# Weight sums of the seven-product groups made in device memory by adding transfers and streamed as pieces, with six groups in each of five down stages

## The chip, the cores and the metric

One core of one Trainium2 chip runs the whole program as a single launch. The metric is the device time of the program in microseconds, the median of several runs. PE is TensorE (its weight loads are listed as PEld), DVE is VectorE, ACT is ScalarE, POOL is GpSimd, SP is the engine that issues most transfers. L941 is line 941 of the kernel before; the changed kernel has other line numbers.

## The reference, cut to what matters

Two transformer blocks on 256 tokens of width 2048, all in float32. The parts that the change touches are the last matrix products of the two feed-forward layers:

```python
# first block, hidden width 8192
h = h + jnp.square(jax.nn.relu(hn @ ffn_w1[i])) @ ffn_w2[i]
...
# second block, hidden width 5632
gate, val = jnp.split(c, 2, axis=-1)        # c: causal convolution of h @ w_up
return (jax.nn.silu(gate) * val) @ w_down
```

Around them stand an attention layer with compression at the start (stages `vs` to `wo`), a gated product (`proj`, `gate`) and a sliding-window attention (`v2` to `wo2`).

## The kernel before

**Precision.** Each float32 operand is split into a high part (the value cast to `fp32r`) and a low part (the value minus its high part). A product of two tiles is three matmuls of 128x512: high by high, high by low, low by high (`product`, L941 to L943). For weights ACT writes the high part (L2157) and DVE the low part (L1307).

**The weight stream.** All weights lie in device memory as `wstream`, a row of 512 KB pieces (128 partitions x 1024 floats). SP loads piece i into one of four `raw` slots (L557) as soon as `lo_ready` says that the low part of piece i-4 is written. ACT casts it to one of four `wboth` slots as soon as `piece_used` says that PE is through with piece i-4; DVE then writes the low part and raises `lo_ready`, for which PE waits. So a piece passes SP, ACT, DVE and PE in this order, on each engine in the order of the stream.

**The stages.** The first feed-forward layer runs in four chunks of 2048 hidden units, c = 0 to 3. Stage `ff{c}` makes 16 hidden tiles from 32 pieces (four passes `it` of four tiles, `units`, L607 and L615; a tile takes two pieces). Stage `fd{c}` multiplies these 16 tiles by 2048 rows of the second weight (32 pieces, each one hidden tile's 128 rows by 1024 columns). The second layer has `up0`, `dn0`, `up1`, `dn1`, `up2`, `dn2`, with 16, 16 and 12 hidden tiles.

**What each hidden tile passes in an `ff` stage.** DVE reduces the two halves of the bank to `z` (L1338), POOL multiplies by the norm factors (L2661, called a take below), ACT applies relu (L2373) and writes the square's high part to H (L2375), POOL squares again (L2708) and writes the low part (L2711). On ACT the casts of the next two pieces stand behind relu and square of a tile; on DVE the reduction of a tile stands between two low parts.

**The seven-product groups.** A down stage is worked in two column halves (`cp` 0 and 1) of 16 pieces. In `plain` a piece costs four products (two token halves by two column halves of 512). Two neighbouring pieces, hidden tiles 2m and 2m+1, cost eight products plainly; a group (`group`) does them with seven, as Strassen's and Winograd's scheme does for a 2x2 block product. It needs sums of the four 128x512 weight tiles (`Tsum`) and sums of the hidden tiles (`mix`, L2746 to L2750 on POOL, high part L2411 on ACT, low part L2756 on POOL). Of the pair's first piece only half is split, since the other half enters in sums alone. Before the change four sums per group are made by DVE or POOL from `raw` (L1777 and L1779, or L2736 and L2738; then L1785 and L1787), cast by ACT (L2418, L2420) and lowered by DVE (L1794). `fd0` to `fd2` have two groups in each column half (m = 3 and 5), `dn0` and `dn1` two and three (m = 4, 6 and m = 2, 4, 6): 22 groups in all. `fd3` and `dn2` have none.

```python
FIRST = Pairing(((3, 5), (3, 5)), sides=12, mains=17, last_sides=28)
SECOND = Pairing(((4, 6), (2, 4, 6)), sides=14, mains=16, last_sides=32)
```

## Time and profile before

| | before |
|---|---|
| median of three runs | 2194.44 us (2193.75 to 2196.51) |
| the profiled execution's own time | 2195.73 us |
| its span in the profile | 2193.9 us |
| PE busy | 2180.1 us, 99% |
| DVE, ACT, POOL busy | 71%, 52%, 32% |
| share of packets of the weight stream's queue | 55.7% of 16 DMA engines |

The profile is of one execution. A busy PE is counted with modelled ends that overlap, so PE's pace is read from the distance of one start to another, not from a matmul's duration. An entry such as `[2.57 <-ACT wboth L2157]` says how long the engine was idle before the instruction and what ended it.

### The profile page before, as it was taken

The numbers are of one execution on the slowest core, as the hardware profiler recorded it, in microseconds if no ns is written. First come the engines' busy times: TensorE is split into PE (matmuls) and PEld (weight loads), VectorE is DVE, ScalarE is ACT, GpSimd is POOL, SyncE is SP. The second block draws the span as 40 slices with busy tenths as digits, with TensorE's granted clock in tenths as the row PEclk, the third lists the DMA queues.
The fourth block names the chain that finished last, engine by engine and source line by source line (L and its number), as shares of the span: only waits on it lengthen the run. The fifth ranks groups of instructions, "written<-read, shape, count | busy, mean of one in ns | idle before, by whom it ended". The sixth has DMA issues, their size and how long they took to land.

```text
span 2193.9 us, 34076 instructions
## 1 busy us (share of the span) xinstructions
PE 2180.1 (99%) x11511; PEld 1862.4 (85%) x11511; DVE 1566.5 (71%) x2187; ACT 1133.5 (52%) x1720; POOL 711.8 (32%) x625
## 2 busy tenths in 40 slices
PE   9999999999999999999999999999999999999998
PEld 7888988888888888888888887788888888888887
DVE  6876767558657757755878667567778777787775
ACT  6445555545445545454556455465455455554553
POOL 3202320361362263153000033005554355533531
PEclk9999999999999999999999999999999999999999
DMA  7665335556556556566565654545555665555664
GB/s 250 231 224 171 116 130 181 174 184 211 191 182 209 192 184 207 202 194 197 177 199 188 225 171 137 192 163 182 189 195 185 202 198 192 188 191 197 200 207 149
DMA packets 118084, 414.35 MB, mean 189 GB/s; under 512 B 12896, under 2 KB 18048, under 8 KB 117472
## 3 DMA queue, kind: packets, MB, share of 16 engines
q1 hardware_dynamic: 111600, 401.37, 55.7%
q10 hardware_dynamic: 6384, 11.70, 1.7%
...
q14 instruction: 43, 0.35, 0.0%
...
## 4 chain that ended last, share of the span: by engine, by line
PE 93%; DVE 4%; ACT 1%; DMA 1%; POOL 1%; issue 1%; SPq 0%; DVEq 0%; ACTq 0%; POOLq 0%
PE bank L607 33%; PE bank L615 17%; PE bank L941 6%; PE bank L943 6%; PE bank L942 6%; PE bank L664 2%; PE bank L666 2%; PE bank L665 2%; DVE wboth L1307 2%; PE bank L1269 1%; PE bank L1267 1%; PE bank L1268 1%; PE bank L740 1%; PE bank L1202 1%; PE bank L777 1%; PE bank L917 1%
## 5 line engine op out<-in xcount | busy, mean ns | idle before, releaser
L1307 DVE TENSOR_TENSOR wboth<-raw,wboth 128x1024 fp32r<-128x1024 f32 (+1 forms) x756 | 953.8, 1267 | 468.1 <-ACT wboth L2157 459.8
L2157 ACT CAST wboth<-raw 128x1024 fp32r<-128x1024 f32 (+1 forms) x756 | 773.0, 1034 | 469.3 <-PE bank L943 123.3
L607 PE MATMUL bank<-A,wboth 128*128 128x512 f32 x2928 | 705.4, 392 | 0.5 <-DVE wboth L1307 0.3
L607 PEld LDWEIGHTS bank<-A,wboth 128*128 128x128 f32 x2928 | 536.8, 188 | 105.3 <-issue 1.3
L615 PEld LDWEIGHTS bank<-A,wboth 128*128 128x128 f32 x2928 | 376.7, 191 | 14.8
L615 PE MATMUL bank<-A,wboth 128*128 128x256 f32 x2928 | 384.0, 283 | 0.0
L941 PE MATMUL bank<-wboth,H 128*128 128x512 f32 x508 | 197.8, 389 | 1.2 <-DVE wboth L1307 1.2
L943 PE MATMUL bank<-wboth,H 128*128 128x512 f32 x508 | 197.6, 389 | 0.0
L942 PE MATMUL bank<-wboth,H 128*128 128x512 f32 x508 | 197.6, 389 | 0.0
L2661 POOL TENSOR_TENSOR PT<-z,rs 128x256 f32<-128x256 f32 x88 | 92.5, 1052 | 263.4 <-DVE z L1338 261.3
L2661 POOL TENSOR_TENSOR bias<-z,rs 128x256 f32<-128x256 f32 x64 | 104.7, 1635 | 197.9 <-DVE z L1338 109.4
L1338 DVE TENSOR_REDUCE z<-bank 128x256 f32<-128x512 f32 x172 | 117.6, 685 | 12.2 <-PE bank L607 12.1
L2373 ACT ACTIVATE Sm<-bias 128x256 f32<-128x256 f32 x64 | 26.7, 418 | 171.2 <-POOL bias L2661 171.2
L941 PEld LDWEIGHTS bank<-wboth,H 128*128 128x128 f32 x508 | 95.4, 188 | 21.8 <-DVE wboth L1307 2.0
L943 PEld LDWEIGHTS bank<-wboth,H 128*128 128x128 f32 x508 | 95.4, 188 | 19.8
L942 PEld LDWEIGHTS bank<-wboth,H 128*128 128x128 f32 x508 | 95.4, 188 | 19.7
L2766 POOL TENSOR_TENSOR x<-x,Sm 128x512 f32<-128x512 f32 x18 | 35.4, 1995 | 206.8 <-DVE x L1841 137.6
L2611 ACT ACTIVATE PT<-PT,par 128x256 f32<-128x256 f32 x88 | 44.8, 509 | 98.0 <-POOL PT L2661 98.0
L2661 POOL TENSOR_TENSOR kT<-z,rs 128x256 f32 (+1 forms) x12 | 11.3, 946 | 248.8 <-DVE z L1338 248.8
L2077 DVE SCALAR_TENSOR_TENSOR Sm<-PT,par 128x256 f32<-128x256 f32 x88 | 50.4, 573 | 51.7 <-ACT PT L2611 51.7
L2805 POOL TENSOR_TENSOR bias<-Sm 128x256 f32<-128x256 f32 x44 | 72.4, 1645 | 39.6 <-DVE Sm L2080 39.3
L607 PE MATMUL bank<-H,wboth 128*128 128x512 f32 x320 | 79.1, 394 | 0.0
...
## 6 DMA issues: line engine op xcount, KB each, us to landing
raw<-wstream SPq DMA_DIRECT2D x756, 512.0 KB, 3.4
bias<-bias_rows ACTq DMA_DIRECT2D x6, 512.0 KB, 5.4
...
pA<-bias_rows ACTq DMA_DIRECT2D x2, 512.0 KB, 6.9
...
```

The lines of the kernel that those rows point to most:

```text
L607: last = nc.tensor.matmul(bank(j)[:, :], whi[:, s, cols(i)], moving(j, k), start=(k == 0), stop=(k == K - 1))
L615: last = nc.tensor.matmul(bank(j)[:, 0:S], wlo[:, s, cols(i)], moving(j, k)[:, 0, :], start=False, stop=False)
L941: nc.tensor.matmul(bank[:, :], a_hi, w_hi, start=start, stop=False)
L942: nc.tensor.matmul(bank[:, :], a_hi, w_lo, start=False, stop=False)
L943: return nc.tensor.matmul(bank[:, :], a_lo, w_hi, start=False, stop=stop)
L1307: V.tensor_tensor(wlo[:, s, 0:w], raw[:, s, 0:w], whi[:, s, 0:w].bitcast(F32), ALU.subtract).then_inc(lo_ready, 1)
L1338: V.tensor_reduce(dst(j) if dst else z[:, (z0 + j) % 4, :], bank[:, :].rearrange("p (h c) -> p c h", h=2), AX, ALU.add).then_inc(z_ready, 1)
L2077: V.scalar_tensor_tensor(tA[:, slot, :], ub[:, slot, 1:S + 1], w[1], c0[:, slot % 2, :], ALU.mult, ALU.add).then_inc(up_step, 1)
L2157: C.copy(whi[:, s, 0:w], raw[:, s, 0:w]).then_inc(hi_ready, 1)
L2611: C.activation(c0[:, j % 2, :], ub[:, j % 4, 0:S], ACT.Copy, scale=par[:, ds(PO["conv"][0] + 3 * (2 * t0 + j), 1)]).then_inc(up_c0, 1)
L2661: return lambda zz: G.tensor_tensor(dst, zz, by, ALU.mult)
L2805: G.tensor_tensor(zr[:, slot + 1, :], tC[:, slot, :], tB[:, slot + 1, :], ALU.mult).then_inc(up_h, 1)
```

## The change

There are now six groups in each of five down stages (m = 2, 4 and 5 in each column half of `fd0`, `fd1`, `fd2`, `dn0`, `dn1`): 30 groups. The sums of weights are no longer made on DVE, POOL and ACT. POOL issues transfers that write them to a tensor `weight_sums` in device memory, in three steps for each group: `sum_copy` copies the two pieces (1 MB), `sum_first` adds the other halves onto them (two adding transfers of 512 KB and 256 KB), `sum_last` adds one sum onto the other two (512 KB). For the stage `fd{c+1}` the copies are issued in `ff{c}`, the first adds in `fd{c}`, the last in `ff{c+1}`; those of `fd0` in the first attention's stages, of `dn0` around `ff3` and `fd3`, the last adds of `dn1` in `gate`. Here the helper index c+1 counts `dn0` and `dn1` as 3 and 4. SP streams the two sums as two more pieces, so a group is four pieces (a full one, a half one, two full ones) where it was two, and a paired stage has 44 pieces where it had 32. Each is split by ACT and DVE as any other piece.

```diff
+FIRST = Pairing(((2, 4, 5), (2, 4, 5)))
+SECOND = Pairing(((2, 4, 5), (2, 4, 5)))
...
+            def load_pairs(c):
+
+                at, fd = pairing(c), stage_at(c)[1]
+                for (cp, m), i in at.begin.items():
+                    w = WB[fd] + 16 * cp + 2 * m
+                    if m in at.fast[cp]:
+                        g = at.used(0) * cp + at.fast[cp].index(m)
+                        load(PB[fd] + i, wstream[w + 1])
+                        load(PB[fd] + i + 1, wstream[w, :, 0:WIDE])
+                        if g == 0:
+                            sp.wait_ge(sums_done, 16 * group_of(c + 1, 0))
+                        for h in range(2):
+                            load(PB[fd] + i + 2 + h, weight_sums[2 * group_of(c, g) + h])
...
+                    arrive(i, 2 * m + 1)
+                    product(main_bank(c, cp, 0), *hidden(2 * m + 1, early), *weights(i, 0))
+                    pe.wait_ge(*mix_ready.at(mix_count(c, at.mixed.index(m) + 1)))
+                    product(main_bank(c, cp, 2), *mix_of(m, 3), *weights(i, 1)).then_inc(piece_used, 1)
                     arrive(i + 1)
+                    product(side_bank(c, cp, ONE), *hidden(2 * m, early), *weights(i + 1, 0), lone, final).then_inc(piece_used, 1)
+                    arrive(i + 2)
+                    product(side_bank(c, cp, FIVE), *mix_of(m, 1), *weights(i + 2, 0), lone, final)
+                    product(side_bank(c, cp, SEVEN), *mix_of(m, 0), *weights(i + 2, 1), lone, final).then_inc(piece_used, 1)
+                    arrive(i + 3)
+                    product(side_bank(c, cp, SIX), *mix_of(m, 2), *weights(i + 3, 1), lone, final).then_inc(t_used.sem, 1)
+                    product(main_bank(c, cp, 1), *hidden(2 * m + 1, late), *weights(i + 3, 0)).then_inc(piece_used, 1)
...
-                    V.tensor_tensor(sums_part(c, 1)[:, two, :], sums_at(c)[:, two, :], sums_part(c, 0)[:, two, :].bitcast(F32), ALU.subtract).then_inc(t_lo.sem, 1)
...
+            def sum_copy(c, g):
+
+                x, n = first_weight(c, g), group_of(c, g)
+                pool.dma_start(weight_sums[2 * n:2 * n + 2], wstream[x:x + 2]).then_inc(sums_copied, 16)
+
+            def sum_first(c, g):
+
+                x, n = first_weight(c, g), group_of(c, g)
+                pool.wait_ge(sums_copied, 16 * group_of(c + 1, 0))
+                pool.dma_start(weight_sums[2 * n].rearrange("p (f w) -> p f w", f=2), wstream[x:x + 2, :, WIDE:].rearrange("a p w -> p a w"),
+                               accum_op=ALU.add).then_inc(sums_half, 16)
+                pool.dma_start(weight_sums[2 * n + 1, :, 0:WIDE], wstream[x + 1, :, WIDE:], accum_op=ALU.add).then_inc(sums_half, 16)
+
+            def sum_last(c, g):
+
+                n = group_of(c, g)
+                pool.wait_ge(sums_half, 32 * group_of(c + 1, 0))
+                if g == 0 and c:
+                    pool.wait_ge(sums_done, 16 * n)
+                pool.dma_start(weight_sums[2 * n + 1].rearrange("p (f w) -> p f w", f=2),
+                               weight_sums[2 * n, :, 0:WIDE].unsqueeze(1).to_broadcast([P, 2, WIDE]), accum_op=ALU.add).then_inc(sums_done, 16)
...
+                    for j in range(2):
+                        if not is_last(c) and 2 * it + j in FIRST.mixed:
+                            mix(c, FIRST.mixed.index(2 * it + j), tB, 2 * j, 2 * j + 1)
+                        g = 2 * it + j
+                        if g < len(pairing(c).groups):
+                            sum_last(c, g)
+                        if g < len(pairing(c + 1).groups):
+                            sum_copy(c + 1, g)
...
+                for g in range(len(pairing(c + 1).groups)):
+                    pool.wait_ge(piece_used, SLOTS + PB[fd] + 2 + 2 * g)
+                    sum_first(c + 1, g)
```

Three places in the order of instructions. The first is POOL in `ff0`, at the end of the third pass (`it` = 2) and the begin of the fourth. Before, the low part of H's last tile of the pass, the mix of hidden tiles 10 and 11 into `kT`, and the next take:

```order
L2711 TENSOR_TENSOR H<-Sm,H 128x256
L2746 TENSOR_TENSOR kT<-Sm 128x256
L2748 TENSOR_TENSOR kT<-kT,Sm 128x128
L2750 TENSOR_TENSOR kT<-Sm,kT 128x128
L2661 TENSOR_TENSOR bias<-z,rs 128x256
```

With the change, at the same place:

```order
L2711 TENSOR_TENSOR H<-Sm,H 128x256
L2735 TENSOR_TENSOR kT<-Sm 128x256
L2737 TENSOR_TENSOR kT<-kT,Sm 128x128
L2739 TENSOR_TENSOR kT<-Sm,kT 128x128
L2686 DMA weight_sums<-weight_sums 256x1x512
L2670 DMA weight_sums<-wstream 16x16384
L2735 TENSOR_TENSOR kT<-Sm 128x256
L2737 TENSOR_TENSOR kT<-kT,Sm 128x128
L2739 TENSOR_TENSOR kT<-Sm,kT 128x128
L2686 DMA weight_sums<-weight_sums 256x1x512
L2670 DMA weight_sums<-wstream 16x16384
L2634 TENSOR_TENSOR bias<-z,rs 128x256
```

Between two takes there stand now two mixes and four issued transfers where one mix stood. The second place is DVE at the begin of `fd0`, behind the last loop of `ff0`. Before, the low parts of pieces 5 and 6 with the first group's sums between and behind them (PT holds the sums, Tboth their parts):

```order
L1307 TENSOR_TENSOR wboth<-raw,wboth 128x1024
L1777 TENSOR_TENSOR PT<-raw 128x512
L1779 TENSOR_TENSOR PT<-raw 128x512
L1307 TENSOR_TENSOR wboth<-raw,wboth 128x512
L1785 TENSOR_TENSOR PT<-PT,raw 128x512
L1787 TENSOR_TENSOR PT<-PT,raw 128x512
L1307 TENSOR_TENSOR wboth<-raw,wboth 128x1024
L1794 TENSOR_TENSOR Tboth<-PT,Tboth 128x1024 x2
```

With the change there are low parts alone, of pieces 5 (half), 6 to 10, 11 (half), 12 to 14, 15 (half), 16 to 21:

```order
L1327 TENSOR_TENSOR wboth<-raw,wboth 128x512
L1327 TENSOR_TENSOR wboth<-raw,wboth 128x1024 x5
L1327 TENSOR_TENSOR wboth<-raw,wboth 128x512
L1327 TENSOR_TENSOR wboth<-raw,wboth 128x1024 x3
L1327 TENSOR_TENSOR wboth<-raw,wboth 128x512
L1327 TENSOR_TENSOR wboth<-raw,wboth 128x1024 x6
```

The first group stands now at the fifth piece of the stage (m = 2) instead of the seventh (m = 3). The third place is POOL at the begin of `fd0`, with the change: the low parts of the three mixes, and behind them the twelve adding transfers for `fd1`, of which four are shown; before, the corrections of x by `corners` (L2766) followed the mixes at once.

```order
L2745 TENSOR_TENSOR mixlo<-kT,vT 128x512 x3
L2676 DMA weight_sums<-wstream 256x1x512
L2678 DMA weight_sums<-wstream 128x512
L2676 DMA weight_sums<-wstream 256x1x512
L2678 DMA weight_sums<-wstream 128x512
```

## Rows read from the trace of the kernel before

**Rows 1.** Page: busy time of the engines, with share of the span

```profile
PE 2180.1 (99%) x11511; PEld 1862.4 (85%) x11511; DVE 1566.5 (71%) x2187; ACT 1133.5 (52%) x1720; POOL 711.8 (32%) x625
```

**Rows 2.** Timeline of PE in fd0: start us, us, line

```profile
484.55 0.39 PE L941 MATMUL bank<-wboth,H 128*128 128x512 f32 x1
...
487.27 0.39 PE L941 MATMUL bank<-wboth,H 128*128 128x512 f32 x1
...
502.95 0.50 PE L941 MATMUL bank<-wboth,H 128*128 128x512 f32 x1 [1.17 <-DVE wboth L1307]
```

**Rows 3.** Timeline of DVE around the begin of fd0

```profile
483.01 1.23 DVE L1307 TENSOR_TENSOR wboth<-raw,wboth 128x1024 fp32r<-128x1024 f32 x1 [2.56 <-ACT wboth L2157]
...
489.69 0.68 DVE L1338 TENSOR_REDUCE z<-bank 128x256 f32<-128x512 f32 x1
...
499.75 0.68 DVE L1307 TENSOR_TENSOR wboth<-raw,wboth 128x512 fp32r<-128x512 f32 x1
...
501.67 1.22 DVE L1307 TENSOR_TENSOR wboth<-raw,wboth 128x1024 fp32r<-128x1024 f32 x1
```

**Rows 4.** Timeline of PE at the begin of fd1

```profile
659.51 0.39 PE L941 MATMUL bank<-wboth,H 128*128 128x512 f32 x1
```

**Rows 5.** Timeline of DVE around the begin of fd1

```profile
655.74 1.23 DVE L1307 TENSOR_TENSOR wboth<-raw,wboth 128x1024 fp32r<-128x1024 f32 x1 [2.57 <-ACT wboth L2157]
...
662.41 0.68 DVE L1338 TENSOR_REDUCE z<-bank 128x256 f32<-128x512 f32 x1
...
672.50 0.68 DVE L1307 TENSOR_TENSOR wboth<-raw,wboth 128x512 fp32r<-128x512 f32 x1
```

**Rows 6.** Timeline of DVE at the end of ff3: the last tile's reduction

```profile
1018.71 0.68 DVE L1338 TENSOR_REDUCE z<-bank 128x256 f32<-128x512 f32 x1
```

**Rows 7.** Timeline of PE at the begin of fd3

```profile
1017.64 0.39 PE L664 MATMUL bank<-wboth,H 128*128 128x512 f32 x1
```

**Rows 8.** Timeline of POOL in ff1, its first take and the second pass

```profile
579.63 0.74 POOL L2661 TENSOR_TENSOR bias<-z,rs 128x256 f32<-128x256 f32 x1
...
617.42 1.65 POOL L2661 TENSOR_TENSOR bias<-z,rs 128x256 f32<-128x256 f32 x1 [1.92 <-DVE z L1338]
...
620.30 0.74 POOL L2711 TENSOR_TENSOR H<-Sm,H 128x256 fp32r<-128x256 f32 x1
620.99 0.75 POOL L2746 TENSOR_TENSOR kT<-Sm 128x256 f32<-128x256 f32 x1
...
623.22 0.47 POOL L2750 TENSOR_TENSOR kT<-Sm,kT 128x128 f32<-128x128 f32 x1
623.64 1.72 POOL L2661 TENSOR_TENSOR bias<-z,rs 128x256 f32<-128x256 f32 x1
...
629.24 1.65 POOL L2661 TENSOR_TENSOR bias<-z,rs 128x256 f32<-128x256 f32 x1 [1.92 <-DVE z L1338]
```

**Rows 9.** Timeline of ACT at the same place

```profile
619.11 0.42 ACT L2373 ACTIVATE Sm<-bias 128x256 f32<-128x256 f32 x1 [2.67 <-POOL bias L2661]
...
625.39 0.42 ACT L2373 ACTIVATE Sm<-bias 128x256 f32<-128x256 f32 x1 [3.42 <-POOL bias L2661]
```

**Rows 10.** Windows: A:B us, busy of PE, PEld, DVE, ACT, POOL, PEclk, DMA share, GB/s

```profile
484.00:574.00 90.00, 88.83 (x399) 73.39 (x398) 72.96 (x80) 45.16 (x51) 16.84 (x12) 1.00 0.62 203
...
20.00:26.00 6.00, 6.00 (x26) 4.22 (x25) 4.03 (x7) 2.95 (x5) 0.00 (x0) 1.00 1.03 401
```

**Rows 11.** Line of SP's loads: ns min/median/max of one issue

```profile
L557 SPq DMA_DIRECT2D raw<-wstream x748: 332/333/587, 18.1 to 2164.2; - x187
```

**Rows 12.** Timeline of POOL at the begin of fd0: two low parts of mixes

```profile
494.63 4.04 POOL L2756 TENSOR_TENSOR mixlo<-kT,vT 128x512 fp32r<-128x512 f32 x2 [0.56 <-ACT vT L2411]
```

**Rows 13.** Page, transfers: KB of one, median us from issue to landing

```profile
raw<-wstream SPq DMA_DIRECT2D x756, 512.0 KB, 3.4
```

**Rows 14.** Page, costliest groups: busy us, mean ns of one

```profile
L1307 DVE TENSOR_TENSOR wboth<-raw,wboth 128x1024 fp32r<-128x1024 f32 (+1 forms) x756 | 953.8, 1267 | 468.1 <-ACT wboth L2157 459.8
L2157 ACT CAST wboth<-raw 128x1024 fp32r<-128x1024 f32 (+1 forms) x756 | 773.0, 1034 | 469.3 <-PE bank L943 123.3
```

More of the change, by code:

```diff
@@ L1405, in take_rs, with rows_body @@
                     dve.wait_ge(rs_ready, then)
-            def rows_body(p, p0, per, groups, evac, between={}, short=0, ahead={}, halves=()):
+            def rows_body(p, p0, per, groups, evac, between={}, short=0, halves=()):
                 for q in range(LEAD, per * groups + AHEAD):
-                    if q in ahead:
-                        ahead[q]()
                     if AHEAD <= q < per * groups + AHEAD - short:
@@ L1796, in sides_in @@
+                rows_body(o * CHP + PB[fd], PB[fd], at.count, 1, lambda f: None, steps_of, halves=at.halves)
             def sides_in(c, cp):
@@ L2698, in _ @@
                     take(UB["q"], ZB["q"], i // 2, mul(y[:, i // 2, :], rs2))
+                if i % 4 == 3 and i // 4 < len(FIRST.groups):
+                    sum_copy(0, i // 4)
+            for g in range(len(FIRST.groups)):
+                pool.wait_ge(piece_used, SLOTS + PB["wo"] + 15 + 2 * g)
+                sum_first(0, g)
             pool.wait_ge(rs_ready, 3)
```

291 lines of the change are left out of this document (118 added, 173 removed).

## The prediction

> **What bounds the kernel now.** I read the page's busy times first: PE is busy 99% of the span and no other engine over 71% [rows 1]. Then the timeline of PE, for its pace and its waits. In a down stage twelve matmuls of 128x512 start in 487.27 - 484.55 = 2.72 us [rows 2], so one takes 0.227 us, a product (three of them) 0.68 us, a plain piece 2.72 us. The only idle time of PE over 1 us in `fd0` is 1.17 us at 502.95, where it waits for a low part of DVE's [rows 2]. So the kernel is a row of matmuls at a fixed pace, and a change pays what it saves in matmuls unless it makes PE wait.
>
> The question is then how far the pieces run ahead of PE. In `fd0` the half piece (the seventh, L1307 with 128x512) is written at 499.75; counted back by six low parts, the stage's first is 483.01 + 1.23 = 484.24 [rows 3], and PE wants it at 484.55 [rows 2]: it is 0.3 us ahead. In `fd1` PE starts at 659.51 [rows 4], and the same count gives 655.74 + 1.23 = 656.97 [rows 5]: 2.5 us ahead. The reduction of the last hidden tile tells the same: it starts 5.1 us after PE has left the tile in `fd0` (489.69 against 484.55), 2.9 us in `fd1` (662.41 against 659.51), so this delay and the lead sum to 5.4 us in both [rows 2 to 5]. In `ff3` the delay is 1.07 us [rows 6, 7], so the lead there is 4.4 us.
>
> What sets the lead in an `ff` stage is a closed loop, as the timelines of POOL and ACT show. The takes of POOL come every 5.6 us (623.64 to 629.24), two pieces' time of PE; POOL is idle 1.92 us before a take, for DVE's reduction [rows 8]; ACT is idle 2.67 us for POOL's take [rows 9]; and DVE is idle 2.57 us for ACT's cast [rows 5]. Since casts stand behind a tile's relu on ACT and reductions behind a low part on DVE, a take that comes late makes the next pieces late. The mix in `ff1` is the trace's own trial of that: POOL works 620.99 to 623.69 for it, 2.70 us, in a gap of 1.92; the take, due at 620.30 + 0.74 + 1.92 = 622.96, starts at 623.64, 0.68 us late [rows 8], and ACT waits 3.42 instead of 2.67 us [rows 9]. So of whatever POOL gets to do between two takes, all over 1.92 us comes out of the lead; and since the loop's period lies close to PE's, little comes back before the stage ends.
>
> **The change part by part.**
>
> (1) Products. 30 groups instead of 22 save eight products: 8 x 0.68 = 5.4 us [rows 2].
>
> (2) DVE loses the sums in the down stages. It was busy 73 of 90 us in `fd0` [rows 10], so this frees an engine on which PE waits there only once, for 1.17 us [rows 2]. I count that wait as gone: 1.2 us.
>
> (3) POOL in the `ff` stages. After passes 0, 1 and 2 it issues four transfers each; mixes follow after pass 1 (one) and pass 2 (two) where each had one. Call D what POOL spends on one issue. No row of before has a transfer issued by POOL. The nearest from below is SP's issue, 0.33 us [rows 11] (or nothing, if POOL only hands it on); the nearest of POOL's own work is 0.47 to 2.02 us for one operation [rows 8, 12]. I take D = 1.0 us, near the middle of POOL's rows, since POOL has to make these descriptors with its own cores. A take that comes late has one relief: it no longer runs beside DVE's low part, and costs 0.74 instead of 1.65 us [rows 8], so 0.9 less. Per stage: pass 0, 4.0 - 1.92 - 0.9 = 1.2; pass 1, 2.70 more, 3.9; pass 2, twice 2.70 more, 6.6; sum 11.7, less the two mixes' 0.68 each that the lead pays already, 10.3 us. From this the lead goes off that is still there at the stage's end: 0.3 us in `ff0`, 2.5 in `ff1`, and I take 2.5 in `ff2`, which runs the same loop body. PE waits 10.0 + 7.8 + 7.8 = 25.6 us. `ff3` has no mixes: 3 x 1.2 = 3.6 us, under its lead of 4.4, nothing. With D = 0.33 the terms are 0, 1.2 and 3.9, less 1.4: 3.7 per stage, in all 3.4 + 1.2 + 1.2 = 5.8 us. With D = 2.0 they are 5.2, 7.9, 10.6: 22.3 per stage, 61.6 in all, and 11 in `ff3`: 73 us.
>
> The Trainium skill (DMA: Bandwidth & Descriptors, Specifications) gives about 1 us to the first byte on the gpsimd path and 0.6 on the sync path. If all of that were POOL's own time the sum would stand as it is; no run here shows it yet.
>
> (4) The first group of `fd0` to `fd2` stands at the fifth piece. PE reaches the first product that needs a mix at 484.55 + 4 x 2.72 + 0.68 = 496.1; POOL ends the first low part of a mix at 494.63 + 2.02 = 496.65 [rows 2, 12]. That is 0.5 us late, and ACT has a third mix to cast among the pieces: I take 0.9 us for each stage, 2.7 in all, since the lead is spent there after (3). In `dn0` and `dn1` I take nothing.
>
> (5) Pieces in a group. A group's seven products last 21 x 0.227 = 4.8 us and use four pieces. A `raw` slot is taken for landing 3.4 us, cast 1.03 and low part 1.27 [rows 13, 14], in all 5.7 us, so each group eats 0.9 us of lead, the neighbours m = 4 and 5 1.9. DVE has 3 x 1.27 + 0.68 = 4.5 us to do in 4.8, so it keeps up and gives nothing back. Between nothing and 1.9 us per pair of groups; I take 0.5 for the seven pairs without adding transfers beside them (second halves of `fd0` to `fd2`, all four of `dn`): 3.5 us.
>
> (6) Transfers that add, in the first half of `fd0` to `fd2`. The highest rate in the trace is 401 GB/s with all 16 engines busy [rows 10]: 1.31 us for a piece, 1.96 for one group's 768 KB if a byte costs once, 3.9 if the destination is read too. While PE passes pieces 2 to 17 (25.2 us), the stream wants 14.5 x 1.31 = 19.0 us and six groups' adds 11.8 to 23.5: 6 to 17 us too much. Much of it can lie behind, in the second half. If the two share the engines evenly a piece takes 2.6 us, which plain pieces (2.72) bear and three groups (3.5 pieces in 4.8 us) don't: at most 3 x 4.4 = 13 us per stage, at least nothing. I take 3 us, since up to four pieces are in flight or landed beforehand: 9 us. The copies and last adds fall into `ff` stages, where the stream asks for one piece in 2.8 us (half of 5.6 [rows 8]) and the casts are POOL's to release; nothing. The stream's share of the engines was 62% in `fd0` [rows 10].
>
> The Trainium skill (DMA: Bandwidth & Descriptors, Issuing engines are not separate DMA queues) says that transfers issued by any engine run on the same 16 DMA engines and interleave. By that rule the adds can't be free beside a stream that a group makes ask for 3.5 x 524 KB in 4.8 us, 382 GB/s; the 401 GB/s row agrees that there is little above it.
>
> Sum: -5.4 - 1.2 + 25.6 + 2.7 + 3.5 + 9 = +34.2 us. Against the profiled execution's own 2195.7 us that is 2229.9; the median of the runs lies 1.3 us lower, so 2228.6.
>
> **The rivals.**
>
> *Faster: POOL's issues are short.* If D is 0.33 or less and (5), (6) are hidden, the sum is -6.6 + 5.8 or less, and at D near nothing only two mixes behind pass 2 are left (5.4 - 1.92 - 0.9 - 1.4 = 1.2, of which `ff0` pays 0.9): 2194.4 - 5.7 = 2189. It decides at D of about 0.35 us, where the POOL term and 1 us of (4) and (5) eat the gain. For it: POOL is idle 68% of the span [rows 1] and may only hand over descriptors. Against it: the mix already overran its gap, so the idle time is in the wrong place. Between this and the next, D of 0.3 to 0.5 gives 2192 to 2199, no change.
>
> *The DMA engines alone.* POOL's issues are cheap, but the adding transfers take the upper end of (6), 13 us in three stages, and 1.9 in each pair: -6.6 + 6 + 39 + 13 = +51, about 2246. For it: 401 GB/s against a need of 380. Against it: the adds have no deadline before the next `ff` stage, so they can trail into the second half, and the landing time of 3.4 us [rows 13] shows no queue today.
>
> *Heavier POOL.* D of 2 us, since an adding transfer has 256 rows: +82 us, 2276.
>
> **How the numbers follow.** The forecast (D between 0.5 and 1.5, moderate contention, 2205 to 2250) has 0.43; the faster rival 0.20; no change 0.09; the DMA engines 0.13; heavier POOL 0.15. A measurement of this kernel tells 0.2%, 4.4 us. Faster is the second alone, 0.20; slower the first, fourth and fifth, 0.71. The range of 2189 to 2268 leaves out some 0.1 of the heavier cases above and some 0.08 of the faster one below; the forecast's own is 2205 to 2250 (D of 0.5 to 1.5 by the same terms, the contention of (6) halved or doubled).
>
> **What would show each step.** (1) A paired `fd` stage has 384 - 18 = 366 matmuls at 0.227 us where it had 372. (3) On POOL, the take behind the issued transfers starts late, ACT's relu waits over 4 us for it, and PE waits for L1327 in `ff0` to `ff2`; the length of a DMA issue on POOL's queue is D, and it is what would make the prediction wrong. (4) PE idle before the first `product` with a mix. (5) and (6) ACT's casts wait for `raw`, landings over 5 us, more in first halves than in second ones.

## The result and the profile after

The changed kernel takes 2301.46 us (median of 4 runs, 2299.34 to 2303.91), the kernel before 2194.61 us (median of four): 1.0486 times as long, 95% interval 1.0468 to 1.0504. The sign was forecast, the size was not: +107 us where the sum said +34, and the time lies above the range (2189 to 2268).

The page of the profile after: busy times, the slices of granted clock and of DMA share, the queues, and the shares of the chain that ended last, which answer to [rows 1] and [rows 13].

```profile
span 2302.1 us, 31629 instructions
PE 2211.7 (96%) x11487; PEld 1863.3 (81%) x11487; DVE 1541.1 (67%) x2131; ACT 1152.4 (50%) x1739; POOL 780.2 (34%) x741
...
PEclk9999999999998999999999999999999999999999
DMA  7676449789789878978978565454656755576564
...
q1 hardware_dynamic: 120240, 424.97, 54.7%
q0 software_dynamic: 21600, 70.79, 13.5%
...
PE 61%; DMA 15%; DVE 9%; POOL 6%; ACT 5%; issue 3%; ACTq 0%; DVEq 0%; POOLq 0%
...
raw<-wstream SPq DMA_DIRECT2D x726, 512.0 KB, 4.2
raw<-weight_sums SPq DMA_DIRECT2D x60, 512.0 KB, 4.5
weight_sums<-wstream POOLq DMA_DIRECT2D x30, 512.0 KB, 15.8
weight_sums<-weight_sums POOLq DMA_DIRECT2D x30, 512.0 KB, 8.9
```

PE runs 24 matmuls fewer (11487), as counted, and ends later. The DMA share stands at 7 to 9 tenths in slices 7 to 22, the first feed-forward layer. A queue that did not exist before moves 70.79 MB for 13.5% of 16 engines' time: 311 us, 4.4 us for each MB, where the stream pays 2302 x 0.547 / 424.97 = 3.0. A piece of the stream lands in 4.2 us at the median (3.4 before), and DMA holds 15% of the last chain, where before PE held nearly all of it.

Where the time went is best read stage by stage, from the first start in each stage in PE's timeline. The rows of the profile after for ff0, fd0, ff1, fd1 and ff2 (start us, us, line):

```profile
392.30 0.39 PE L630 MATMUL bank<-A,wboth 128*128 128x512 f32 x1
...
496.02 0.39 PE L964 MATMUL bank<-wboth,H 128*128 128x512 f32 x1
...
599.11 0.40 PE L630 MATMUL bank<-A,wboth 128*128 128x512 f32 x1
...
700.60 0.39 PE L964 MATMUL bank<-wboth,H 128*128 128x512 f32 x1
...
803.22 0.39 PE L630 MATMUL bank<-A,wboth 128*128 128x512 f32 x1
```

So `ff0` lasts 103.7 us, `fd0` 103.1, `ff1` 101.5, `fd1` 102.6. All stage lengths below are taken in this way, in us:

| kernel | time | ff0 | fd0 | ff1 | fd1 | ff2 | fd2 | ff3 | fd3, gate | dn0 | dn1 |
|---|---|---|---|---|---|---|---|---|---|---|---|
| before | 2194.6 | 90.6 | 85.9 | 89.1 | 84.3 | 89.1 | 84.3 | 89.2 | 199.4 | 83.8 | 83.9 |
| after | 2301.5 | 103.7 | 103.1 | 101.5 | 102.6 | 99.2 | 104.0 | 91.9 | 208.4 | 86.1 | 89.0 |
| e1_no_sums | 2219.3 | 92.3 | 89.3 | 89.2 | 94.1 | 89.1 | 89.5 | 89.2 | 199.4 | 85.9 | 88.4 |
| e2_small | 2237.7 | 98.1 | 90.2 | 96.3 | 90.5 | 94.6 | 91.5 | 89.2 | 199.3 | 88.3 | 86.7 |
| e3_no_first | 2259.2 | 102.8 | 91.7 | 99.0 | 91.6 | 99.7 | 88.6 | 91.6 | 200.5 | 87.7 | 87.5 |
| e4_first_only | 2259.6 | 92.2 | 104.6 | 89.1 | 103.6 | 89.1 | 98.5 | 89.2 | 200.5 | 87.5 | 89.2 |
| e16_adds_in_ff | 2221.4 | 94.2 | 89.1 | 89.1 | 93.8 | 89.4 | 90.7 | 89.2 | 199.3 | 86.0 | 86.4 |
| e6_spread_issue | 2266.3 | 92.5 | 104.1 | 89.1 | 104.4 | 89.2 | 104.8 | 89.2 | 202.3 | 88.2 | 89.0 |
| e11_spread_adds | 2280.1 | 94.2 | 111.0 | 89.4 | 109.6 | 89.6 | 106.2 | 89.2 | 199.5 | 87.2 | 86.1 |
| e7_plain_first | 2284.6 | 102.6 | 98.4 | 99.6 | 101.7 | 100.0 | 98.6 | 89.6 | 204.7 | 87.5 | 86.7 |
| e8_row_copy | 2281.0 | 100.1 | 101.5 | 96.9 | 100.0 | 97.4 | 98.6 | 89.2 | 203.7 | 89.8 | 86.8 |
| e12_all | 2275.9 | 90.8 | 111.5 | 90.9 | 106.0 | 90.7 | 105.7 | 89.2 | 199.4 | 87.1 | 85.3 |
| e5_apart | 2227.9 | 91.4 | 92.7 | 89.2 | 91.7 | 89.1 | 92.0 | 89.2 | 199.3 | 87.2 | 86.6 |
| e9_246 | 2222.6 | 90.6 | 91.0 | 89.2 | 89.2 | 89.2 | 91.0 | 90.8 | 199.4 | 88.1 | 87.3 |
| e10_narrow | 2208.6 | 92.3 | 87.9 | 89.1 | 88.0 | 89.1 | 87.9 | 89.2 | 199.4 | 87.5 | 84.5 |
| e14_bunch_before | 2203.3 | 93.8 | 85.9 | 90.2 | 86.0 | 90.1 | 86.0 | 89.2 | 199.3 | 83.8 | 84.4 |
| e15_spread_before | 2193.7 | 90.5 | 85.8 | 89.1 | 84.3 | 89.1 | 84.3 | 89.2 | 199.3 | 84.0 | 83.9 |

After less before: 35.6 us in `ff0` to `ff2`, 55.2 in `fd0` to `fd2`, 2.7 in `ff3`, 9.0 in `fd3`, 7.4 in `dn0` and `dn1`. The other stages lose nothing (`ff0` starts 1.6 us sooner). Two kinds of stall make it up.

**In an ff stage.** Timelines of the profile after, in `ff0`: POOL behind the second pass, then ACT, then PE (in brackets the idle time before and what ended it). [Rows 8, 9] are the like of before.

```profile
448.31 1.72 POOL L2735 TENSOR_TENSOR kT<-Sm 128x256 f32<-128x256 f32 x1
450.11 1.38 POOL L2737 TENSOR_TENSOR kT<-kT,Sm 128x128 f32<-128x128 f32 x1
451.57 0.47 POOL L2739 TENSOR_TENSOR kT<-Sm,kT 128x128 f32<-128x128 f32 x1
451.97 1.03 POOL L2686 DMA_DIRECT2D weight_sums<-weight_sums  x1
452.58 0.94 POOL L2670 DMA_DIRECT2D weight_sums<-wstream  x1
453.08 1.52 POOL L2686 DMA_DIRECT2D weight_sums<-weight_sums  x1
453.66 1.45 POOL L2670 DMA_DIRECT2D weight_sums<-wstream  x1
454.18 1.69 POOL L2634 TENSOR_TENSOR bias<-z,rs 128x256 f32<-128x256 f32 x1
...
455.90 0.42 ACT L2356 ACTIVATE Sm<-bias 128x256 f32<-128x256 f32 x1 [7.04 <-POOL bias L2634]
456.45 0.42 ACT L2358 ACTIVATE H<-Sm 128x256 f32 x1
456.77 1.97 ACT L2140 CAST wboth<-raw 128x1024 fp32r<-128x1024 f32 x2
...
459.19 3.47 PE L630 MATMUL bank<-A,wboth 128*128 128x512 f32 x8 [3.08 <-DVE wboth L1327]
```

The four issues take 454.18 - 451.97 = 2.21 us, so D, what POOL gives up for one, is 0.55 us, not 1.0. The mix and the issues together keep the take back; ACT stands at the relu for 7.04 us (before 2.67, behind a mix 3.42), with two landed pieces behind it whose casts start at 456.77; PE waits 3.08 us. And the wait costs more than itself. Windows of the profile after, behind this wait and behind the next one of 4.83 us (busy of PE, PEld, DVE, ACT, POOL, then PEclk, DMA share, GB/s):

```profile
459.20:462.50 3.30, 3.30 (x9) 2.63 (x10) 1.59 (x2) 0.96 (x3) 2.24 (x2) 0.55 0.78 208
488.20:492.00 3.80, 3.80 (x10) 3.03 (x11) 1.60 (x2) 1.44 (x3) 2.64 (x3) 0.50 1.14 301
511.00:558.00 47.00, 37.29 (x141) 27.12 (x140) 25.17 (x23) 16.46 (x18) 16.62 (x16) 0.93 1.06 278
558.00:599.00 41.00, 39.33 (x170) 31.12 (x169) 31.15 (x33) 21.97 (x23) 2.15 (x1) 1.00 0.79 260
```

The granted clock is 0.55 and 0.50 there, the lower of the two levels (1.2 GHz): PE had been idle 3 to 5 us before, and its eight matmuls behind the wait take 3.3 and 3.6 us where eight of 0.227 take 1.8. Not every wait is followed by this: in `fd2` PE is idle for 3.10 us before 931.61, and the granted clock stays at 1.00.

```profile
931.60:935.00 3.40, 2.62 (x10) 1.88 (x11) 1.23 (x1) 1.66 (x2) 0.00 (x0) 1.00 1.10 279
```

**In a paired stage.** The third of the windows above is the first half of `fd0`. The twelve first adds are all issued within 14 us; from 511 to 558 us the engines are fully taken (1.06), PE is busy 37.3 of 47 us; from 558 on, with the adds gone, 39.3 of 41. ACT, then PE, in the second group (m = 4):

```profile
521.64 0.62 ACT L2140 CAST wboth<-raw 128x512 fp32r<-128x512 f32 x1 [5.73 <-DMA raw<-wstream]
524.25 1.04 ACT L2140 CAST wboth<-raw 128x1024 fp32r<-128x1024 f32 x1 [1.99 <-DMA raw<-weight_sums]
527.01 1.04 ACT L2140 CAST wboth<-raw 128x1024 fp32r<-128x1024 f32 x1 [1.72 <-DMA raw<-weight_sums]
...
526.60 0.50 PE L964 MATMUL bank<-wboth,vT 128*128 128x512 f32 x1 [2.60 <-DVE wboth L1327]
526.94 0.56 PE L965 MATMUL bank<-wboth,vT 128*128 128x512 f32 x1
527.30 0.63 PE L966 MATMUL bank<-wboth,mixlo 128*128 128x512 f32 x1
527.73 0.63 PE L964 MATMUL bank<-wboth,vT 128*128 128x512 f32 x1
```

ACT waits for landings (it waited for PE or a take before), each passes on to DVE's low part and to PE, and behind the wait the matmuls start 0.34 to 0.43 us apart instead of 0.23. How long loads take, by SP's line of loads in the profile after, `ff0` and then `fd1`, from issue to landing:

```profile
DMA to landing us min/median/max: 3.0/4.4/11.0
...
DMA to landing us min/median/max: 3.2/5.4/10.5
```

### The profile page after: what moved, and what is told of

Read it like the earlier page. It is cut to its first block, busy times and chain, and to the rows that moved or that the text cites. A ratio compares the mean times of both kernels' runs of the same rounds, so it can differ in the third digit from the quotient of the medians.

```text
span 2302.1 us, 31629 instructions
## 1 busy us (share of the span) xinstructions
PE 2211.7 (96%) x11487; PEld 1863.3 (81%) x11487; DVE 1541.1 (67%) x2131; ACT 1152.4 (50%) x1739; POOL 780.2 (34%) x741
## 3 DMA queue, kind: packets, MB, share of 16 engines
q1 hardware_dynamic: 120240, 424.97, 54.7%
q0 software_dynamic: 21600, 70.79, 13.5%
## 4 chain that ended last, share of the span: by engine, by line
PE 61%; DMA 15%; DVE 9%; POOL 6%; ACT 5%; issue 3%; ACTq 0%; DVEq 0%; POOLq 0%
PE bank L630 21%; PE bank L638 11%; DMA raw<-wstream 11%; DVE wboth L1327 5%; ACT wboth L2140 4%; DMA raw<-weight_sums 3%; PE bank L964 2%; PE bank L966 2%; PE bank L965 2%; POOL bias L2634 2%; PE bank L687 2%; PE bank L689 2%; PE bank L688 2%; DVE z L1452 1%; POOL weight_sums L2686 1%
## 5 line engine op out<-in xcount | busy, mean ns | idle before, releaser
L1327 DVE TENSOR_TENSOR wboth<-raw,wboth 128x1024 fp32r<-128x1024 f32 (+1 forms) x816 | 1028.1, 1266 | 609.6 <-ACT wboth L2140 605.5
L2140 ACT CAST wboth<-raw 128x1024 fp32r<-128x1024 f32 (+1 forms) x816 | 834.0, 1031 | 604.4 <-DMA raw<-wstream 192.1
L630 PE MATMUL bank<-A,wboth 128*128 128x512 f32 x2928 | 716.0, 395 | 23.9 <-DVE wboth L1327 23.8
L964 PE MATMUL bank<-wboth,H 128*128 128x512 f32 x490 | 194.8, 398 | 17.9 <-DVE wboth L1327 17.5
L965 PE MATMUL bank<-wboth,H 128*128 128x512 f32 x490 | 191.9, 392 | 0.0
L966 PE MATMUL bank<-wboth,H 128*128 128x512 f32 x490 | 191.7, 391 | 0.0
L2634 POOL TENSOR_TENSOR bias<-z,rs 128x256 f32<-128x256 f32 x64 | 94.0, 1469 | 159.0 <-DVE z L1358 123.6
L964 PEld LDWEIGHTS bank<-wboth,H 128*128 128x128 f32 x490 | 92.8, 189 | 47.4 <-DVE wboth L1327 19.7
L1358 DVE TENSOR_REDUCE z<-bank 128x256 f32<-128x512 f32 x172 | 117.6, 684 | 10.6 <-PE bank L630 10.2
L966 PEld LDWEIGHTS bank<-wboth,H 128*128 128x128 f32 x490 | 92.6, 189 | 19.8
L965 PEld LDWEIGHTS bank<-wboth,H 128*128 128x128 f32 x490 | 92.6, 189 | 18.5
L2584 ACT ACTIVATE PT<-PT,par 128x256 f32<-128x256 f32 x88 | 44.8, 509 | 99.6 <-POOL PT L2634 99.6
L687 PE MATMUL bank<-wboth,H 128*128 128x512 f32 x192 | 76.0, 396 | 7.9 <-DVE wboth L1327 7.9
```

Source lines behind the costliest of these rows:

```text
L630: last = nc.tensor.matmul(bank(j)[:, :], whi[:, s, cols(i)], moving(j, k), start=(k == 0), stop=(k == K - 1))
L687: nc.tensor.matmul(bank[:, :], src[:, k, 0, tok], whi[:, s, w], start=(k == 0), stop=False)
L964: nc.tensor.matmul(bank[:, :], a_hi, w_hi, start=start, stop=False)
L965: nc.tensor.matmul(bank[:, :], a_hi, w_lo, start=False, stop=False)
L966: return nc.tensor.matmul(bank[:, :], a_lo, w_hi, start=False, stop=stop)
L1327: V.tensor_tensor(wlo[:, s, 0:w], raw[:, s, 0:w], whi[:, s, 0:w].bitcast(F32), ALU.subtract).then_inc(lo_ready, 1)
```

## The experiments

Fifteen kernels ran, in four sets, each beside the kernel before (2194.3 to 2195.3 us in the four). Ratios are to it, with their 95% interval.

### What is left without the transfers, and with small ones

**e1_no_sums.** The streamed sums are replaced by plain pieces, and the four transfers of `sum_copy`, `sum_first` and `sum_last` are gone (the first is shown):

```diff
-                        load(PB[fd] + i + 2 + h, weight_sums[2 * group_of(c, g) + h])
+                        load(PB[fd] + i + 2 + h, wstream[w + h])
-                pool.dma_start(weight_sums[2 * n:2 * n + 2], wstream[x:x + 2]).then_inc(sums_copied, 16)
```

> The changed kernel without any transfer on GpSimd's queue: the sums are not made, and the queue streams the plain weight pieces in the places of the two sums, so the outputs of the five paired stages are wrong. Groups, their order, the number and size of the streamed pieces and every other instruction stay. Theory 1 (the cost lies in the 120 adding and copying transfers, by their traffic or by their issue): the paired stages fall from 103 us to 83 to 85 us, the first stages from 99 to 104 us to 89 to 91 us, and the time is 2183 to 2195 us. Rival (the new order of four pieces to a group with a ring of four slots cannot keep TensorE fed by itself): the paired stages stay above 95 us and the time above 2240 us.

2219.28 us, 1.0106 (1.009 to 1.0123). Neither theory: `ff1` and `ff2` are back at 89 us and `ff0` at 92.3, so nearly all of their loss comes from the transfers; but `fd0` to `fd2` keep 3.4 to 9.8 us each, `dn0` and `dn1` 2.1 and 4.5. The new order of pieces costs 24.3 us by itself, although it has eight products fewer: 31 us gross. In PE's timeline of `fd0` the first group has two late starts:

```profile
498.66 0.50 PE L961 MATMUL bank<-wboth,vT 128*128 128x512 f32 x1 [1.14 <-DVE wboth L1324]
...
500.89 0.49 PE L961 MATMUL bank<-wboth,vT 128*128 128x512 f32 x1 [0.57 <-DVE wboth L1324]
```

**e2_small.** The same with the transfers kept, cut to a sixteenth: `weight_sums` has rows of 64 floats, `sum_copy` takes `[:, 0:PW]` of 16 rows, the adds `WIDE:WIDE + 32`.

> The changed kernel with all 120 transfers on GpSimd's queue kept in number, place and waits, each cut to a sixteenth of its bytes (the rows get shorter, their number in the adds stays); the plain pieces are streamed in place of the sums, so the outputs are wrong. Theory 1a (in the first stages the loss is GpSimd's issuing, about 0.55 us each in the trace after, 4 behind each of three passes, in the closed loop of take, relu and cast; in the paired stages it is traffic): first stages 96 to 100 us, paired stages 84 to 86 us, time 2212 to 2230 us. Theory 1b (traffic is all of it): first stages 89 to 91 us, the time within 5 us of the kernel without these transfers. Rival (the number of descriptors is what costs): both kinds of stage stay near their length after, over 2270 us.

2237.66 us, 1.0188 (1.0171 to 1.0205). The transfers without their bytes cost 18.4 us over e1, and this stands in the ff stages (+5.7, +7.1, +5.6), while the paired ones as a whole keep e1's length (272.2 against 272.9 us in `fd0` to `fd2`). 1b and the rival are refuted. 1a is right in its place and its kind, not in all its figures: `ff2` falls below the range it gave, the paired stages (90 to 91 us) and the time lie above, since the cost of the order was not in it.

**e3_no_first** and **e4_first_only** split the traffic. e3 drops both transfers of `sum_first` (the diff); e4 drops those of `sum_last` and, for c > 0, of `sum_copy`, and its `sum_first` adds onto `weight_sums[2 * g]`.

```diff
-                pool.wait_ge(sums_half, 32 * group_of(c + 1, 0))
+                pool.wait_ge(sums_copied, 16 * group_of(c + 1, 0))
...
-                pool.dma_start(weight_sums[2 * n + 1, :, 0:WIDE], wstream[x + 1, :, WIDE:], accum_op=ALU.add).then_inc(sums_half, 16)
```

> The changed kernel without the 60 first adds (two for each group, issued in a burst at the start of fd0 to fd3 and before ff0); copies and last adds stay where they are, and the two stored pieces are streamed as now, so the sums and the outputs are wrong. Theory 1 (the burst of adds fills the DMA engines from 511 to 558 us and sets the pace of the paired stages): the paired stages fall from 103 us to 83 to 86 us and fd3 by 8 us, the first stages stay at 99 to 104 us, time 2228 to 2240 us. Rival (the streamed sums or the order of pieces hold the paired stages): paired stages stay over 95 us, time over 2265 us.

2259.15 us, 1.0289 (1.0272 to 1.0306). The paired stages fall to 88.6 to 91.7 (theory 1 gave 83 to 86, again without the cost of the order), the ff stages keep their loss. Copies and last adds cost 2259.2 - 2219.3 = 39.9 us.

> The changed kernel with only the first adds of each stage and the six copies of the attention stage; the other copies and all last adds are left out, the first adds go onto six stored pairs that are used again in each stage, and the plain pieces are streamed in place of the sums, so the outputs are wrong. Theory 1: the paired stages stay at 101 to 104 us, the first stages fall from 99 to 104 us to 89 to 91 us, time 2262 to 2272 us. Rival (the ff stages lose by what the paired stages before leave late): ff1 and ff2 stay above 97 us.

2259.60 us, 1.0295 (1.0278 to 1.0312). The other way round: `ff1` and `ff2` at 89, `ff0` at 92.2 as in e1, paired stages at 98.5 to 104.6. First adds cost 40.3 us. In the whole the two add up, 39.9 + 40.3 = 80.2 of the 82.2 us between e1 and the changed kernel; in single stages they don't: `fd3` loses 1.2 us in either and 9.0 with both. That ff stages lose by what a paired stage leaves late is refuted.

### The bunch of issues in the ff stages

**e6_spread_issue.** All bytes move, all sums are made; only the place of the issues changes:

```diff
                         G.tensor_tensor(part(H, it * 4 + j, 1), ...).then_inc(ff_ready, 1)
+                        g = 4 * it + j - 4
+                        if 0 <= g < len(pairing(c).groups):
+                            sum_last(c, g)
+                        elif 0 <= g - 6 < len(pairing(c + 1).groups):
+                            sum_copy(c + 1, g - 6)
```

> The changed kernel (2301.5 us) with the twelve transfers of an ff stage (six last adds, then six copies) issued one behind each of tiles 4 to 15 instead of four behind each of three passes; all sums are made in full. Theory 1a (issuing in a bunch behind a mix holds up the take, the relu and the casts queued behind it; it was 5.6 to 7.5 us of each ff stage in the run with small transfers): ff0 to ff2 fall from 103.7, 101.5 and 99.2 us to 93 to 98 us, time 2280 to 2292 us. Rival (bytes, not issues, cost the ff stages): ff stages stay at 99 to 104 us and the time at 2296 to 2306 us.

2266.34 us, 1.0333 (1.0308 to 1.0358): 35 us off, more than 1a gave, since the ff stages are as long as in e1, and all that the transfers cost them is gone. Windows of `ff1` and `fd1`, columns as above, and SP's loads of `ff1`:

```profile
588.00:677.00 89.00, 89.00 (x511) 78.48 (x510) 47.73 (x49) 40.58 (x59) 59.79 (x62) 1.00 0.82 248
677.00:782.00 105.00, 92.78 (x374) 70.47 (x373) 63.78 (x62) 49.23 (x56) 31.14 (x29) 0.95 0.94 290
```

```profile
DMA to landing us min/median/max: 3.1/5.5/9.6
```

With DMA at 0.82 and landings of 5.5 us (median) PE is busy 89 of 89 us. A tile's gap of 1.92 us takes one issue of 0.55. So neither the bytes nor the count of issues costs these ff stages anything; four issues in front of one take do, the more so while landings are long (e2 against the changed kernel: +6 against +12).

**e14_bunch_before** and **e15_spread_before** put the same question to the kernel before, with small transfers of no use, in e14 four behind each of passes 0 to 2, in e15 one behind each of tiles 4 to 15:

```diff
+                pool.dma_start(small_to[n], wstream[0:2, :, 0:32].rearrange("a p w -> p a w")).then_inc(scratched, 16)
```

> The kernel before, all its work done, with 48 small transfers added on GpSimd's queue (256 rows of 128 bytes each, to a tensor that nothing reads): four behind each of the first three passes of ff0 to ff3, where the changed kernel issues its own. GpSimd's loop over the chunks is written out for it. Theory 1a (a bunch of four issues, about 2.2 us, in front of the next take is what the ff stages lose, with or without traffic and groups): each ff stage 4 to 8 us longer, time 2208 to 2225 us. Rival 1c (the kernel before hides 2.2 us a pass, and the loss needs the late leads of the new order): under 2 us for each ff stage, time 2193 to 2201 us.

2203.25 us, 1.0044 (1.0027 to 1.0061). POOL, then ACT, behind its second pass:

```profile
448.19 0.46 POOL L2758 TENSOR_TENSOR kT<-Sm,kT 128x128 f32<-128x128 f32 x1
448.59 2.68 POOL L2705 DMA_DIRECT2D small_to<-wstream  x4
450.81 1.23 POOL L2663 TENSOR_TENSOR bias<-z,rs 128x256 f32<-128x256 f32 x1
...
452.08 0.42 ACT L2375 ACTIVATE Sm<-bias 128x256 f32<-128x256 f32 x1 [5.15 <-POOL bias L2663]
```

Here too four issues take 2.22 us, and the relu waits 5.15 instead of 3.42 us. `ff0` to `ff2` lose 3.2, 1.1 and 1.0 us, `fd1` and `fd2` behind them 1.6 each. That is between the two theories: under the 4 to 8 us a stage of 1a, and over 1c in `ff0` and in the time. So the bunch costs without the new order too, but less. That one mix a pass stands with it, not two, and that the lead of 2.5 us pays a part in `ff1` and `ff2`, fits the lengths; it was not tested by itself.

> The kernel before with the same 48 small transfers, one behind each of tiles 4 to 15 of ff0 to ff3. Theory 1a (one issue of 0.55 us fits into the 1.9 us that GpSimd waits for the next tile): no stage changes by over 0.5 us, except where a mix stands, time 2193 to 2199 us. Rival 1d (the count of issues costs, wherever they stand): ff stages as long as in the bunched run.

2193.74 us, 0.9999 (0.999 to 1.0009): no stage of the table moves by over 0.3 us. The same 48 issues are free, one to a tile.

### The adds in the paired stages

**e7_plain_first** takes `accum_op=ALU.add` out of both transfers of `sum_first`.

> The changed kernel (2301.5 us) with the 60 first adds as plain copies of the same rows to the same places, so the sums and outputs are wrong: as many transfers, packets and written bytes, without the add. Theory 3a (a 2 KB packet that adds occupies a DMA engine for 176 to 194 ns against 84 for a plain one of its size, and this occupied time is what the streamed pieces lack): the paired stages fall from 103.1, 102.6 and 104.0 us to 94 to 99 us, fd3 from 208.4 to 203 to 206, time 2276 to 2290 us. Rival 3b (the count of packets or the bytes cost, the add as such is free): no stage changes by over 2 us, time 2296 to 2306 us.

2284.63 us, 1.0405 (1.0388 to 1.0422). As many rows asked for and bytes written; `fd0` to `fd2` lose 1 to 5.4 us less each and `fd3` 3.7, so 3a holds but for `fd1` (101.7, above its 94 to 99). On the page of the profile the queue's share falls from 13.5% of 2302 us to 10.6% of 2283, 69 us less for 23.6 MB of first adds:

```profile
q0 software_dynamic: 15840, 70.79, 10.6%
```

(The page counts 5760 packets fewer, since the plain rows went two and two as packets of 4 KB.) At the stream's 3.0 us for a MB the 23.6 MB would take 71 us, so the add doubles what a byte occupies. About 17 us of the time come from it; the rest of the adds' 40 us does not, as far as numbers from two kernels can be set against each other.

**e8_row_copy** makes each copy `"a p w -> p a w"` on both sides.

> The changed kernel (2301.5 us) with each copy of a pair of pieces cut into 256 rows of 4 KB instead of 16 of 64 KB; the same bytes, all sums made in full. Theory 4a (a packet of 64 KB holds its DMA engine for 2.4 to 2.6 us and each streamed piece whose packets stand behind lands later by up to that, beyond the share of its bytes): ff stages fall by 2 to 5 us each, time 2287 to 2296 us. Rival 4b (the occupied time of the engines is all that counts, and more descriptors cost GpSimd more): ff stages stay within 1.5 us or get longer, time 2297 to 2310 us.

2280.99 us, 1.0398 (1.0381 to 1.0415): 20 us off, as 4a gave for the ff stages (-3.6, -4.6, -1.8) and more than it gave in the whole, since `fd2` and `fd3` gain 5 us each. POOL gains nothing: a copy of 256 rows holds it for 0.72 us (450.70 - 449.98), one of 16 rows for 0.5 (452.58 to 453.08 above).

```profile
449.98 1.12 POOL L2670 DMA_DIRECT2D weight_sums<-wstream  x1
450.70 1.47 POOL L2686 DMA_DIRECT2D weight_sums<-weight_sums  x1
```

Rows of 4 KB at equal bytes disturb the stream less than rows of 64 KB.

**e11_spread_adds** releases a group's first adds each six pieces of the paired stage, on top of e6:

```diff
-                    pool.wait_ge(piece_used, SLOTS + PB[fd] + 2 + 2 * g)
+                    pool.wait_ge(piece_used, SLOTS + PB[fd] + (2 + 6 * g if g < 3 else 8 + 6 * g))
```

(in `fd3` at 32/44 of these; `corners` are moved between, so that they don't wait for an add's release).

> The kernel with the ff transfers spread over the tiles (2266.3 us), with the first adds of a paired stage released one group each six pieces over the whole stage instead of in one burst at its start; all sums are made in full. Theory 6a (the burst costs because it leaves a piece no share of the engines for 45 us on end): fd0 to fd2 fall from 104.1, 104.4 and 104.8 us to 93 to 99 us, time 2235 to 2256 us. Rival 6b (the whole stage is short of occupied engine time, 0.94 to 0.95 of the stage in the run before, so that it matters little where the adds stand): fd stages stay at 101 to 106 us, time 2258 to 2270 us.

2280.13 us, 1.0387 (1.0369 to 1.0404): 14 us **worse** than the burst. Both theories fail: `fd0` takes 111.0 us. SP's loads in `fd1` land in:

```profile
DMA to landing us min/median/max: 2.9/6.9/10.7
```

against 6.0 in the burst's run. The likely reading is that the burst hurts for half a stage and the spread adds for all of it.

**e16_adds_in_ff** moves the adds of e4 to the tiles 4 to 15 of the ff stage ahead, one transfer behind each.

> The kernel with first adds only (2259.6 us; outputs wrong as there), with these adds moved out of the paired stages into the ff stage ahead of them, one transfer behind each of tiles 4 to 15. Theory 7a (a transfer costs where the streamed pieces are wanted faster than they can land beside it: ff stages want 32 pieces in 89 us and have room, paired stages want 41 full pieces in 83 us and have none): ff stages stay at 89 to 91 us, paired stages fall from 98 to 105 us to the 89 to 94 us of the run without transfers, time 2217 to 2228 us. Rival 7b (adds of 28 us of occupied engines cost the same wherever they stand): the loss moves to the ff stages, which take 98 to 104 us, time 2250 to 2265 us.

2221.44 us, 1.0124 (1.0107 to 1.0141). The same 60 adds cost 2.2 us over e1 with 48 of them in `ff0` to `ff3`, and 40.3 in e4 with these 48 in `fd0` to `fd3`, 36 of them in paired stages; those in `fd2` are for `dn0`, those in `fd3` for `dn1`, and the twelve for `fd0` stand ahead of `ff0` in both. Its windows of `ff1` and `fd1`:

```profile
575.20:664.20 89.00, 89.00 (x514) 78.64 (x513) 47.12 (x49) 41.89 (x60) 62.11 (x64) 1.00 0.78 223
664.20:758.00 93.80, 87.62 (x370) 69.37 (x369) 64.07 (x62) 47.89 (x55) 20.02 (x15) 0.98 0.78 247
```

7a holds (but for `ff0`, 94.2 us, where e1 has 92.3): what counts is the rate at which the stage wants its pieces. An estimate of how long a landing may take: a `raw` slot is taken for landing plus 2.3 us of cast and low part, and there are four. An ff stage wants a piece each 2.8 us, so landing may take 4 x 2.8 - 2.3 = 8.9 us; a paired stage wants 44 in 83 us, so it may take 4 x 1.886 - 2.3 = 5.2 on the mean, and inside a group (four in 4.8 us) 2.5, which no landing meets. Measured medians are 5.5 in e6's `ff1` (no loss) and 5.4, 6.0 and 6.9 us in `fd1` of the changed kernel, e6 and e11 (102.6, 104.4 and 109.6 us). The estimate tells which stage has room, not how much one without it loses: at 4.4 us, under the mean of 5.2, `fd1` of e1 still takes 94.1 us, and no run changed the number of slots.

### The order of the pieces by itself

**e5_apart** and **e9_246** are e1 with other pairs (`FIRST` and `SECOND`); e9 also moves the step that follows the second half's last group (`over`) one piece forward.

> The kernel without any sum transfer (2219.3 us) with the groups of seven at pairs 1, 3 and 5 of each half instead of 2, 4 and 5, so that no two groups follow each other; nothing of the amount of work changes, and the outputs are wrong as there. Theory 2a (a group takes 3.5 pieces in 4.8 us, which is more than the queue lands, so two groups in a row empty the ring of four slots; a plain pair between refills it): fd0 to fd2 fall from 89.3, 94.1 and 89.5 us to 83 to 86 us, dn1 from 88.4 to 84 to 86, time 2193 to 2203 us. Rival 2b (the mean rate over the whole stage, 41 pieces of 512 KB in 83 us, is what the stream cannot keep): fd stages stay at 88 to 94 us and the time at 2214 to 2224 us.

2227.88 us, 1.0161 (1.0144 to 1.0178): slower than e1, so 2a fails. PE's timeline of `fd0` shows two places:

```profile
495.13 0.79 PE L961 MATMUL bank<-wboth,vT 128*128 128x512 f32 x1 [5.04 <-POOL mixlo L2732]
...
539.76 0.50 PE L961 MATMUL bank<-wboth,H 128*128 128x512 f32 x1 [2.13 <-DVE x L1821]
```

The mix of pair 1 is not ready, and the side banks are wanted too early in the second half. Elsewhere in `fd0` no start is late by over 0.5 us, so single groups are borne, but the pairs that allow it cost elsewhere.

> The kernel without any sum transfer (2219.3 us; outputs wrong as there) with groups at pairs 2, 4 and 6 of each half. In the run with pairs 1, 3 and 5 the pieces inside the stages came at least 0.7 us ahead of TensorE, and what it lost stood at two places: 5.2 us before the first group, whose mixes were late, and 2.3 us where the second half's first group follows the change of banks. Theory 2c (single groups between plain pairs cost nothing, two in a row do, and a group at pair 1 comes before its mix): fd0 to fd2 take 84 to 87 us instead of 89.3, 94.1 and 89.5, time 2200 to 2212 us. Rival 2b (the mean rate of the stage costs, wherever the groups stand): 88 to 94 us, time 2214 to 2226 us.

2222.64 us, 1.0119 (1.0101 to 1.0136): as e1, 89 to 91 us a stage. 2c fails and 2b's figures hold; the loss changes its places, not its size.

**e10_narrow** is e1 with `wstream[w + h, :, 0:WIDE]` for the sums' two pieces.

> The kernel without any sum transfer (2219.3 us; groups at 2, 4, 5) in which the two pieces of each group that stand for the sums are fetched as 256 KB instead of 512 KB; their other halves keep what the ring's slot held, casts and subtractions keep their full width, and the outputs are wrong. Theory 5a (landing, 4.2 to 6.6 us inside two groups in a row, empties the ring): fd0 to fd2 fall to 84 to 87 us, time 2200 to 2212 us. Rival 5b (cast and subtraction, 1.03 and 1.27 us a piece behind each landing, or the waits for mixes and side banks hold it, whatever the bytes): fd stages within 1.5 us of 89.3, 94.1 and 89.5 us, time 2214 to 2224 us.

2208.64 us, 1.0062 (1.0045 to 1.0078): `fd0` to `fd2` at 87.9 to 88.0, so 5b is refuted and 5a's stages come out 1 us short. Of the 24.3 us the landing of full pieces is 10.6. What stays, 4.8 us over 83.1 in each, stands in PE's timeline of `fd1` as starts that come late by 1.3 and 0.7 us in the first group and by 1.3 and 1.1 at the pairs in a row.

**e12_all** joins e11, the rows of e8 and pairs 2, 4, 6.

> All helpful edits together, with all sums made in full: issues spread over the tiles, copies in rows of 4 KB, first adds spread over the stage, groups at pairs 2, 4 and 6. Theory (the costs add: 2301.5 less 35 for spreading the issues, less 10 to 30 for the first adds, less 5 to 10 for the rows, less 8 to 15 for the groups): 2215 to 2243 us, so still slower than the kernel before at 2194.6 us. Rival (the costs overlap, the engines' occupied time sets the paired stages whatever the order): 2246 to 2266 us.

2275.88 us, 1.0369 (1.0352 to 1.0386). That is above both ranges. The gains don't add: `fd0` takes 111.5 us, as with the spread adds of e11. The best kernel that makes all sums is e6, 2266 us.

## Why the prediction was right in sign and wrong in size

- **(1) and (2), -6.6 us.** Right as far as counted: 24 matmuls fewer, 5.4 us, and no sums on DVE; the 1.2 us of (2) no run measures by itself.
- **(3), 25.6 us, POOL's issues.** The mechanism is right and shown (relu waits 7.04 us, e2, e14, and e6 takes it away). D was 0.55 us, not 1.0; the issues alone cost 18.4 us. That 25.6 comes near is in part luck. With D at 0.55 the terms are 0, 2.1 and 4.8, less 1.4: 11.2 us in three stages. The relief of 0.9 us was misread: the late take behind the mix in [rows 8] lasts 1.72 us, and the one behind the bunch shown above 1.69, not 0.74. Without it in the first two passes the terms give 14.7; the other 4 us are open.
- **(6), "the copies and last adds ... nothing".** This failed. In the same places, full bytes of copies and last adds cost 21.5 us more (e3 less e1, 39.9) than e2's small ones (18.4). The argument (a piece in 2.8 us leaves room) was right for a stage with spread issues, as e6 shows; it failed because the bunch had already used up the slack that long landings need. Two disturbances were priced each as if it had the lead for itself.
- **(6), 9 us for the first adds.** Mis-sized: 40.3. Its own upper bound, 13 us in each of three stages, was near the truth: e4 less e1 is 15.3, 9.5 and 9.0 us in `fd0` to `fd2`. I took 3 because pieces landed beforehand would bridge it, but the adds fill the engines for 47 us, three times as long as the eight pieces in the two rings last (8 x 1.89 = 15 us).
- **(4) and (5), 6.2 us.** Mis-sized: 30.9. (4) gave 0.9 for each first group; the two late starts there add to 2.0 us in `fd0` of e1. (5) took landing at 3.4 us, the median before; a stage that streams 41 instead of 32 pieces' bytes in the same time lands in 4.4 (e1), and e10 shows that 10.6 us hang on this. The rest is waits at groups in a row, which the closed form "5.7 against 4.8" called 1.9 for two in a row; the sum then took a quarter of it.

By the runs the sum is -6.6 + 30.9 (order, e1) + 18.4 (issues, e2) + 21.5 (bytes of copies and last adds beside them, e3) + 40.3 (first adds, e4) = +104.5, of the 106.5 us from the kernel before in the set of e1 (2194.98) to the changed kernel (2301.46). The third and fourth terms rest on e3 and e2 as they are; e2 has the small first adds as well, e3 has none. The step that failed most is (6): contention was given 9 us of a true 62. Of the rivals "the DMA engines alone" had the right place and its upper end of (6), but no bunch; those that rest on D, of 0.33 or of 2 us, are refuted by 0.55.

The Trainium skill (DMA: Bandwidth & Descriptors, Issuing engines are not separate DMA queues) says that transfers of all issuers interleave on the same 16 engines. The runs agree: in e4 adds issued by POOL make `fd0` to `fd2`, fed by SP's stream, 9 to 15 us longer than in e1. That this need cost next to nothing, e16 shows (2.2 us).

What stays open: why rows of 64 KB cost 20 us more than rows of 4 KB with the same occupied time, and how much of the adds' 40 us is queueing in the engines and how much PE's lower clock behind some of the waits. Neither was separated. The mean granted clock of the profiled executions bounds the second: 0.998 before and 0.990 after, so at most some 0.008 x 2302 = 18 us of the 107. No kernel with these groups beat the kernel before; even without any transfer they are 1.1% slower, so a version that only moves the transfers can't win.
